# Single steps for constants, gates, head norms and turns, and VectorE for the rotation's sum

## The reference

```python
oa = diff_attention(...)      # group 0: two softmaxes per head, p0 - lam*p1; rms_norm of the output
ob = window_attention(...)    # group 1: rope, band mask, sink, 2 key heads
on = neighborhood_attention(...)  # group 2: relative bias, 4 key heads
od = qknorm_attention(...)    # group 3: rms_norm of q and k, rope, 2 key heads
y = (jnp.concatenate([oa, ob, on, od], axis=-1) * jax.nn.silu(p[12])) @ w_out[l]

def apply_rope(x, cos, sin):
    h = x.shape[-1] // 2
    x1, x2 = x[..., :h], x[..., h:]
    return jnp.concatenate([x1 * cos - x2 * sin, x2 * cos + x1 * sin], axis=-1)
```

## Time and profile before

| | us |
|---|---|
| median of 3 timed runs | 3154.34 (3153.6 to 3158.98) |
| profiled execution, its own time | 3150.2 |
| its span | 3148.0 |
| TensorE matmul busy | 2928.6 (93%) |
| VectorE busy | 1927.3 (61%) |
| ScalarE busy | 1166.4 (37%) |
| GpSimd busy | 385.0 (12%) |
| mean granted TensorE clock | 0.953 of full speed |

### The profile page before, as it was taken

How to read it: one execution, slowest core, us unless ns; L and a number is a source line. 1 busy time by engine, 2 the same in 40 slices (tenths; PEclk the granted TensorE clock), 3 DMA queues, 4 the chain that set the end, 5 groups by cost and what they waited for, 6 DMA issues and landing times. The chain is left out here.

```text
span 3148.0 us, 40440 instructions
## 1 busy us (share of the span) xinstructions
PE 2928.6 (93%) x15557; PEld 2369.7 (75%) x15557; DVE 1927.3 (61%) x3369; ACT 1166.4 (37%) x1870; POOL 385.0 (12%) x365
## 2 busy tenths in 40 slices
PE   7979899999889996999998998989999999999998
PEld 2447578777667874868776787765789999999886
DVE  3228778676776767262434557886776666666444
ACT  3233332323223334242433444233344444444443
POOL 5760000000100001000000002542410000000000
PEclk9989999999899998999999998995799999999999
DMA  9836235343344664323332353430244555555554
GB/s 339 278 138 238 84 133 197 112 163 121 110 161 148 207 224 151 114 91 112 118 106 96 119 182 126 141 112 22 79 145 151 187 182 182 183 181 188 195 188 156
DMA packets 154592, 484.79 MB, mean 154 GB/s; under 512 B 17168, under 2 KB 18192, under 8 KB 153232
## 3 DMA queue, kind: packets, MB, share of 16 engines
q1 hardware_dynamic: 139968, 439.42, 41.4%
q10 hardware_dynamic: 14432, 42.79, 3.9%
HBM read 469.03 MB, written 13.11 MB: 153 GB/s over the span
## 5 line engine op out<-in xcount | busy, mean ns | idle before, releaser
L1457 DVE TENSOR_TENSOR split_weights<-common,split_weights 128x1024 fp32r<-128x1024 f32 x644 | 798.0, 1247 | 666.3 <-ACT split_weights L2166 611.3
L2166 ACT ACTIVATE split_weights<-common 128x1024 fp32r<-128x1024 f32 x644 | 671.6, 1052 | 829.5 <-PE bank L1133 777.0
L1131 PE MATMUL bank<-split_weights,features 128*128 128x512 f32 x1920 | 806.2, 420 | 27.8 <-DVE split_weights L1457 11.3
L1133 PE MATMUL bank<-split_weights,features 128*128 128x512 f32 x1920 | 759.7, 396 | 0.0
L1132 PE MATMUL bank<-split_weights,features 128*128 128x512 f32 x1920 | 759.3, 395 | 0.0
L1131 PEld LDWEIGHTS bank<-split_weights,features 128*128 128x128 f32 x1920 | 368.4, 192 | 137.7 <-issue 44.3
L1132 PEld LDWEIGHTS bank<-split_weights,features 128*128 128x128 f32 x1920 | 368.7, 192 | 79.3 <-issue 11.3
L1133 PEld LDWEIGHTS bank<-split_weights,features 128*128 128x128 f32 x1920 | 366.6, 191 | 80.6
L1131 PE MATMUL bank<-ffn_input_split,split_weights 128*128 128x256 f32 (+1 forms) x1376 | 389.1, 283 | 0.8 <-issue 0.8
L1133 PE MATMUL bank<-ffn_input_split,split_weights 128*128 128x256 f32 (+1 forms) x1376 | 388.2, 282 | 0.0
L1132 PE MATMUL bank<-ffn_input_split,split_weights 128*128 128x256 f32 (+1 forms) x1376 | 387.7, 282 | 0.0
(11 more groups left out here) (296 smaller groups left out, 3429.5 us busy)
## 6 DMA issues: line engine op xcount, KB each, us to landing
common<-w_in SPq DMA_DIRECT2D x260, 512.0 KB, 3.3
common<-w_up SPq DMA_DIRECT2D x172, 512.0 KB, 4.3
first_block_work<-w_mod_cols SPq DMA_DIRECT2D x256, 256.0 KB, 3.7
common<-w_out SPq DMA_DIRECT2D x104, 512.0 KB, 3.3
common<-w_down SPq DMA_DIRECT2D x84, 512.0 KB, 3.3
old_stream<-w_mod SPq DMA_DIRECT2D x64, 512.0 KB, 5.1
trig<-common ACTq DMA_DIRECT2D x32, 272.0 KB, 5.0
second_block_work<-trig ACTq DMA_DIRECT2D x32, 272.0 KB, 2.7
```

The source lines that it names most:

```text
L1131: e.matmul(out_ap, xs[0], ws[0], start=first, stop=False)
L1133: return e.matmul(out_ap, xs[0], ws[1], start=False, stop=last)
L1457: e.tensor_tensor(lo, raw, hi.bitcast(F32), ALU.subtract).then_inc(*low_done.tick(("lo", m)))
L2166: e.activation(split_slots[:, 0, i, 0:words], raw_slots[:, m % RAW, 0:words], ACT.Copy).then_inc(*high_done.tick(("high", m)))
```

## The change

Four composite steps are taken apart. `layer_consts` becomes `lambda_sums`, `lambda_exp`, `lambda_made` and four `bias_mask` steps, put 20 to 48 sides after the constants' load; the lambda products are written over their own input rather than into a turn buffer. `gate` becomes `gate_tanh` (ScalarE, at the finish) and `gate` (VectorE, two sides later). `norm_heads` becomes `square_heads` (squares, mean, power) at the finish and `norm_heads` with `rotate_heads` two sides later, with two buffers for the means. `heads_out` of group 0 keeps the mean and the power; `heads_scaled`, issued after the next scores, does the scalings and frees bank 7.

The end of q no longer forces the pending turns: it issues the attention that is left and nothing else. Head tiles of group 0's first q and k in layer 0 are turned 20 sides after their finish in place of 3 or 8. Squares and rotations have each their own turn buffer.

In `rotate_heads` the first sine product is multiplied by -1 in the same instruction (a scalar_tensor_tensor), and VectorE adds the whole product tile to the cosine tile in one instruction; GpSimd's two instructions are gone.

```diff
@@ -218,8 +218,8 @@
 
 PACE, LAST_PACE = (0.36, 0.45), (0.65, 0.8)
 SCAN_PACE = 0.5
-CONTEXT_AFTER = 4
-TURN_AFTER = dict(copy=3, turn=8, norm=14)
+CONTEXT_AFTER, GATE_AFTER, NORM_AFTER = 4, 2, 2
+TURN_AFTER = dict(first=20, copy=3, turn=8, norm=14)
 
 
...
@@ -282,11 +283,22 @@
 
     def later(self, sides, *step):
         self.delayed.append((self.clock + sides, step))
+        self.delayed.sort(key=lambda d: d[0])
+
+    def late(self):
+        step = self.delayed.pop(0)[1]
+        if step[0] == "gate":
+            self.scale_heads()
+        self.do(*step)
+
+    def flush(self):
+        while self.delayed:
+            self.late()
 
     def side(self, work=1.0):
         self.clock += 1
         while self.delayed and self.delayed[0][0] <= self.clock:
-            self.do(*self.delayed.pop(0)[1])
+            self.late()
         if self.turned:
             if self.turned[0][0] < self.clock:
                 self.do(*self.turned.pop(0)[1])
...
@@ -493,16 +505,17 @@
             self.staged += 1
             self.stage_before[r], self.stage_now[t] = self.stage_now[t], ("staged", r)
             self.stage_last[(l, t)] = ("staged", r)
-            after = "copy"
+            after = "first" if l == 0 and g == 0 else "copy"
             if kind == "qk":
                 self.scratch += 1
-                self.do("norm_heads", l, g, part, nh, p, t, bank, r, self.turns(), self.scratch)
+                self.do("square_heads", l, nh, p, t, bank, r, self.turns(0))
+                self.later(NORM_AFTER, "norm_heads", l, part, nh, t, r, self.scratch)
                 if t < LT:
-                    self.do("rotate_heads", l, nh, "head", p, t, bank, r, self.turns(), self.scratch)
+                    self.later(NORM_AFTER, "rotate_heads", l, nh, "head", p, t, bank, r, self.turns(1), self.scratch)
                 after = "norm"
             elif t < LT and ROPE[kind]:
-                self.do("rotate_heads", l, nh, ROPE[kind], p, t, bank, r, self.turns(), None)
-                after = "turn"
+                self.do("rotate_heads", l, nh, ROPE[kind], p, t, bank, r, self.turns(t % 2), None)
+                after = "first" if l == 0 and g == 0 else "turn"
             else:
                 self.do("copy_heads", l, g, part, nh, p, t, bank, r)
             self.turned.append((self.clock + TURN_AFTER[after], ("turn_heads", l, g, part, nh, t, r)))
...
@@ -545,13 +559,21 @@
                 t, h = units[i - 2]
                 self.do("values", first + i - 2, l, g, kvh, t, h)
                 if h == HEADS - 1:
+                    self.flush()
                     r = None
                     if ("gate", l, g, t) in self.reached:
                         r = self.rows()
                     else:
                         self.reached.add(("output", l, g, t))
                     self.do("heads_out", first + i - 2, l, g, kind, t, r)
+                    if kind == "diff":
+                        self.unscaled.append(("heads_scaled", first + i - 2, l, g, t, r))
             yield
+        self.scale_heads()
+
+    def scale_heads(self):
+        while self.unscaled:
+            self.do(*self.unscaled.pop())
 
     def gate(self, l, g):
         def finish(p, t, bank):
...
@@ -560,7 +582,8 @@
                 r = self.rows()
             else:
                 self.reached.add(("gate", l, g, t))
-            self.do("gate", l, g, p, t, bank, r)
+            self.do("gate_tanh", l, g, p, t, bank, r)
+            self.later(GATE_AFTER, "gate", l, g, p, t, bank, r)
         return finish
 
     def y_rows(self, l, c, at):
...
@@ -581,7 +604,8 @@
                         self.project(tiles[LT:], self.heads(l, g, kind, "k", HEADS))
                 elif part == "q":
                     self.project(qtiles, self.heads(l, g, kind, "q", HEADS))
-                    self.side_all()
+                    while self.side_work:
+                        self.advance(self.side_work)
                 elif part == "k":
                     self.project(tiles, self.heads(l, g, kind, "k", HEADS))
                 elif part == "v":
...
@@ -591,9 +615,11 @@
                 if g == 0 and part == "q":
                     self.scratch += 1
                     self.do("load_layer_consts", l, self.scratch)
-                    mask_at = self.scratch
-            if g == 0:
-                self.do("layer_consts", l, mask_at, self.turns())
+                    self.later(20, "lambda_sums", l)
+                    self.later(26, "lambda_exp", l)
+                    self.later(32, "lambda_made", l)
+                    for h in range(HEADS):
+                        self.later(36 + 4 * h, "bias_mask", l, h, self.scratch)
             self.side_work.append(self.attention(l, g, kind, kvh, qtiles))
             self.pace = PACE[l] if place < 3 else LAST_PACE[l]
             self.project(qtiles, self.gate(l, g))
...
@@ -1630,36 +1657,40 @@
             e.tensor_tensor(feat[:, 1, f, 0:nt * P], tb[:, 0:nt * P], feat[:, 0, f, 0:nt * P].bitcast(F32), ALU.subtract).then_inc(
                 *features_made.tick(("feature", "mixed", l, f, 0), ("feature", "mixed", l, f, 1), ("free", "mixed", l, f)))
 
-        def layer_consts(l, z, x):
-            m = scratch.rearrange("p (t k) -> p t k", k=LAT)
+        def bias_mask(l, h, z):
             for s, n in seen.new(at("bias", l), at("mask", l)):
                 e.wait_ge(s, n)
-            for h in range(HEADS):
-                b = na_bias[:, h * LT:(h + 1) * LT, :]
-                names = [("na_ready", l), ("scratch", z)] * (h == HEADS - 1)
-                e.tensor_tensor(b, b, m, ALU.add).then_inc(*constants_made.tick(*names))
+            b = na_bias[:, h * LT:(h + 1) * LT, :]
+            names = [("na_ready", l), ("scratch", z)] * (h == HEADS - 1)
+            e.tensor_tensor(b, b, scratch.rearrange("p (t k) -> p t k", k=LAT), ALU.add).then_inc(*constants_made.tick(*names))
+
+        def lambda_sums(l):
             lv = lam_words.rearrange("p (v d) -> p v d", d=SUB)
-            prod = (turn_a, turn_b)[x % 2][:, 0:2 * SUB].rearrange("p (v d) -> p v d", d=SUB)
-            for s, n in seen.new(at("lambdas", l), at("turn", x - 2)):
-                e.wait_ge(s, n)
-            e.tensor_tensor(prod, lv[:, 0:3:2, :], lv[:, 1:4:2, :], ALU.mult).then_inc(*constants_made.tick())
+            for s, n in seen.new(at("lambdas", l)):
+                e.wait_ge(s, n)
+            e.tensor_tensor(lv[:, 0:3:2, :], lv[:, 0:3:2, :], lv[:, 1:4:2, :], ALU.mult).then_inc(*constants_made.tick())
             e.wait_ge(*constants_made.last())
-            e.tensor_reduce(lam_t[:, 0:2], prod, AX.X, ALU.add).then_inc(*constants_made.tick(("lambda_sums", l)))
+            e.tensor_reduce(lam_t[:, 0:2], lv[:, 0:3:2, :], AX.X, ALU.add).then_inc(*constants_made.tick(("lambda_sums", l)))
+
+        def lambda_made(l):
             for s, n in seen.new(at("lambda_exp", l)):
                 e.wait_ge(s, n)
             e.tensor_tensor(lam_col, lam_t[:, 2:3], lam_t[:, 3:4], ALU.subtract).then_inc(*constants_made.tick())
             e.wait_ge(*constants_made.last())
             e.tensor_scalar(lam_col, lam_col, 0.8 - 0.6 * math.exp(-0.3 * l), None, ALU.add).then_inc(
-                *constants_made.tick(("lambda", l), ("turn", x)))
-
-        def norm_heads(l, g, part, nh, p, t, bank, r, x, z):
-            w = nh * HD
-            src, hs, gain = stage[t][:, 0:w], hss[:, 0:nh], 0 if part == "q" else 1
+                *constants_made.tick(("lambda", l)))
+
+        def square_heads(l, nh, p, t, bank, r, x):
+            w, hs = nh * HD, head_sums[r % 2][:, 0:nh]
             for s, n in seen.new(at("head_squares", r)):
                 e.wait_ge(s, n)
             e.tensor_reduce(hs, h3((turn_a, turn_b)[x % 2][:, 0:w]), AX.X, ALU.add).then_inc(*heads_made.tick(("turn", x)))
             e.wait_ge(*heads_made.last())
             e.tensor_scalar(hs, hs, 1.0 / HD, EPS, ALU.mult, ALU.add).then_inc(*heads_made.tick(("head_means", r)))
+
+        def norm_heads(l, part, nh, t, r, z):
+            w = nh * HD
+            src, hs, gain = stage[t][:, 0:w], head_sums[r % 2][:, 0:nh], 0 if part == "q" else 1
             for s, n in seen.new(at("head_power", r), at("scratch", z - 1)):
                 e.wait_ge(s, n)
             e.tensor_tensor(h3(scratch[:, 0:w]), h3(src), bc(hs, 2, (P, nh, HD)), ALU.mult).then_inc(*heads_made.tick())
...
@@ -1686,9 +1717,13 @@
             e.tensor_tensor(a, v, cos, ALU.mult).then_inc(*heads_made.tick())
             for s, n in seen.new(at("turn", x - 2)):
                 e.wait_ge(s, n)
-            e.tensor_tensor(b[:, :, 0, :], v[:, :, 1, :], sin, ALU.mult).then_inc(*heads_made.tick())
+            e.scalar_tensor_tensor(out=b[:, :, 0, :], in0=v[:, :, 1, :], scalar=-1.0, in1=sin, op0=ALU.mult, op1=ALU.mult).then_inc(
+                *heads_made.tick())
             names = [("free", "acc", p, t)] if z is None else [("scratch", z)]
```

(47 more changed lines are left out.)

51 lines of the change are left out of this document (27 added, 24 removed).

## The result

The changed kernel takes 3111.6 us (median of 4, 3109.5 to 3112.07), the kernel before on the same chip 3153.97 (4 runs, 3150.27 to 3158.98): ratio 0.9863, interval 0.9846 to 0.988, 42.4 us faster. Forecast were 3097, 57 us faster. The profiled execution of the changed kernel spans 3110.3 us, 37.7 less than before's.

What follows compares the result with a forecast made beforehand. TensorE, busy 93% of the span, was taken as the bound (at most some 220 us to be had). Seven terms summed to 57.1 us, span 3148.0 to 3090.9; with 2.2 and 4.1 added, 3097 us, range 3060 to 3125.

Steps and rivals of the forecast that it cites:

- 1 first turns: Layer 0's first head turns: later turns let TensorE restart sooner after its 14.1 us wait; 6.7 us gained, bounds 4 to 8.
- 2 constants: First attention, layer 0: masks and lambda in single steps shorten VectorE's lateness; 2.5 us gained, bounds 0 to 8.
- 3 difference heads: Difference attention's tile ends: later scaling brings the combination sooner, 0.4 us at each of six; 2.5 us, bounds -3 to 9.
- 4 window group, layer 0: Layer 0's window group: key products fill the gap after q as far as VectorE follows; 5.4 us, bounds 2 to 10.6.
- 5 norm group, layer 0: Layer 0's norm group: the gap after q fills as far as VectorE's queue shortens; 11 us, bounds 5 to 22.7.
- moved pieces: Seven modulation pieces moved to later stages shift one load of c rows into the stream's end; ±2 us, taken as 0.
- 6 layer 1: Layer 1's three ends of q: VectorE has room, so the gaps really fill; 28 us gained, bounds 20 to 31.
- step 7: Turns of copied heads after q, now spread; 1 us gained.
- the stalls move: Rival, 3118 us, chance 0.24: in layer 0 TensorE waits the same later, at the end of kv or a weight split.
- all gaps fill: Rival, 3068 us, chance 0.14: VectorE catches up while TensorE works; layer 0's window and norm groups give 33.3 us, not 16.4.
- The sums: All 24 rotations, with sums moved from GpSimd, were charged as 15.1 us more work for VectorE.
- The slower rival: Rival, 3188 us, chance 0.07: the gate frees its accumulator two steps later, delaying projections at 24 gate tiles, 91 us.

Runs made afterwards that it cites:

- Experiments 2: The kernel before with one part alone: the end of q no longer forces the turns, sums stay on GpSimd; 3132.57 us, ratio 0.9927.
- experiment 4: The changed kernel with `side_all` back at the end of q, forcing the turns again; 3136.38 us, ratio 0.9939 to the kernel before.
- experiment 3: The changed kernel with the sums of the rotated heads back on GpSimd; 3115.89 us, ratio 0.9875 to the kernel before.
- experiment 12: The kernel before with 64 modulation pieces held back to layer 1 and one piece in 4 sides in layer 0; 3120.88 us, ratio 0.9892.
- Experiment 7: The changed kernel with 1, 3 and 5 modulation pieces put in at layer 0's three ends of q; 3117.19 us, ratio 0.9881.
- Experiment 8: The changed kernel with the last 64 modulation pieces (layer 1's gates) held back until layer 1's attention; 3092.84 us, ratio 0.9808.
- experiment 11: The changed kernel with the last 64 modulation pieces held back and one piece in 4 sides instead of 3 without attention work; 3059.44 us, ratio 0.9694.
- experiment 9: The changed kernel with the difference heads scaled at once, in the step of the heads' output; 3117.38 us, ratio 0.9874.
- experiment 10: The changed kernel with the gate's second half and the norm due at the next side, not two later; 3115.99 us, ratio 0.9872.

## Why the prediction was right, and where it was off

By its own steps, in us of the two profiled spans (37.7 in all; the medians differ by 42.4). Each is the rise in the changed kernel's column between two products.

| step | forecast | measured | between products |
|---|---|---|---|
| 1 first turns | 6.7 | 4.9 | start to 129 |
| 2 constants | 2.5 | 1.7 | 183 to 202 |
| 3 difference heads | 2.5 | 1.6 | 202 to 276 |
| 4 window group, layer 0 | 5.4 | 4.7 | 520 to 697 |
| 5 norm group, layer 0 | 11 | 6.5 to the end of kv, 11.1 to the attention's | 697 to 837, to 896 |
| moved pieces | 0 (±2) | -11.9 | 896 to 1183 |
| 6 layer 1 | 28 | 24.9 | 1183 to 1796 |

What is left: -0.4 from 129 to 183, 2.6 from 276 to 520 (the copied heads' turns of step 7, forecast 1, and further difference heads), and -1.5 after the attention.

The measured 3111.6 lies inside the stated range of 3060 to 3125, but 1.6 above the forecast's own 3085 to 3110, and nearer to the rival "the stalls move" (3118) than to 3097. That is chance: this rival gives terms 2 to 5 nothing, and they gave 19.1 us (forecast 21.4). A loss that no term of the sum held brought the total down to it.

**The mechanism held.** Experiments 2 and 4 show it from both sides: letting q end without its forced turns is worth 20 to 25 us, the rest of the change 17 to 19 (experiment 4 against its before). The size that steps 4 and 5 set, what TensorE keeps if VectorE must follow, came out too: 15.8 us by the attention's end for 16.4 forecast, with 12.4 of 34.0 us given back in the norm group's kv. The rival "all gaps fill" wanted 33.3 us from them. It was wrong for this kernel, and no less for the paced one, where the change gives these two groups 15.3 us. So 16 pieces fewer (150 for 166 at product 896) did not make the change worth more there, nor did the sums taken off VectorE in experiment 3 (16.2 us). VectorE's work is on TensorE's path in these groups in both kernels: the pacing alone gives 18.3 us from product 520 to 896 (experiment 12). That it is also what stops the gaps from filling rests on the waits shown, for VectorE or for ScalarE behind VectorE, and not on an experiment.

**The step that failed is "The seven pieces moved to later ... ±2, taken as 0".** They came to 9 by product 896 (175 against 166), not seven, each of two passes, and the term cost 11.9 us. I had credited steps 4 and 5 with the pieces that leave, and not debited the stage that they go to. The code's order told where: the output projection, in which VectorE is busy 147.07 of 204.12 us before and waits 33.4 us for the next pieces' loads from 985 to 1215. Experiment 4 removes the loss by bringing back the whole old order. Experiment 7, which brings back the number of pieces and not their places, shows two parts: about 6.9 us with the moved pieces, and 4.2 with the one that stands ahead of the features. Experiment 8 shows that the stage is better off still without the last 64. Of the 6.2 us c-row load only its new place and the longer wait (10.52 for 7.24) are shown; I did not try the load alone.

**Step 6 was too high in its first group:** 5.9 (14.3 to 20.2) where 9.9 were forecast. The column reaches 24.9 at product 1186 and loses 4.7 at once. VectorE, still at the features, rotates late, and TensorE stops 2.03 us and runs slow:

```profile
1237.79 0.41 DVE L1720 SCALAR_TENSOR_TENSOR common<-bank,first_block_work 128x256 f32<-128x256 f32 x1
1238.12 0.41 DVE L1723 TENSOR_TENSOR common<-bank,first_block_work 128x256 f32<-128x256 f32 x1
...
1238.59 0.50 PE L1158 MATMUL bank<-split_weights,features 128*128 128x512 f32 x1 [2.03 <-DVE common L1723]
```

In experiment 11, with no pieces there, the same group rises from 65.6 to 75.2, 9.6 us. The window group's 5.4 (forecast 4.0) and the norm group's 12.8 (14.4) are right.

**Small terms.** Step 1 was 1.8 high, of which 1.4 is that later stage: taken from there, the restart comes 4.8 us sooner, as forecast, and the slow stretch remained. The sums cost about what I charged: 14.5 us for all 24 against 15.1, a wide one taking 0.69 us, while VectorE's busy time as a whole rose by 10.5. The sine product with the turned sign took as long as the plain one behind it (0.415 us both, 128x256). Step 3's price was shown by experiment 9, by place and not in the total (2.7 us, mine 2.5), with the wait for the scaling at the values that I named. The slower rival, the gate's late accumulator, did not appear: the products wait 0.4 us once behind its line 1850, and experiment 10 without the delay is not faster.

**A rule that spoke against the change.** The Trainium skill, Perfetto Trace Analysis, section Optimizing Scalar/DVE Operations, says that giving work of a saturated VectorE to another engine, even GpSimd, may make sense, with the caution that the two share a read port, so that moving work between them might not help. Here the sums on GpSimd (experiment 3) came out 4 us slower if anything. Between products 520 and 896, where VectorE is fullest, its profile gained 16.2 us and the changed kernel's 15.8, so there it made no difference, and the caution is what this case bears out. GpSimd's 128x256 sums took 1.12 and 1.04 us on the mean, the shortest 0.74 and the longest 1.74. That a port is the reason no run here shows.

## What to carry to other kernels

When an order of work is paced by a counter, taking empty steps out of it moves all that the counter pays out. Price it at the stage that it lands in, not only at the one that it leaves, look at which item now stands ahead of which reader (one piece ahead of two features: 4 to 5 us), and check whether the work was due there at all: 64 pieces that were first needed a layer later cost 17 us by being early, more than most edits of the change gave. Two changes need not add up (42 and 34 us apart, 96 together); where the surplus lies is read from the places, not from the totals. And compare two traces by when the same work is reached, since waits change their names without changing their cost (42.9 us on GpSimd became 36.1 on VectorE, for 1 to 4 us).

## What I had not expected of the hardware

Where VectorE is behind, TensorE can pay for its work in full. In experiment 11 ten pieces fewer by product 697 (118 for the changed kernel's 128) went with 16.5 us gained there (31.6 for 15.1), 1.6 us a piece. That is just what such a piece costs VectorE: two passes of 0.75 us and two reads of 0.08. VectorE was busy only 73% of layer 0's attention before the change, and still none of this work was hidden. The same ten pieces fewer in the kernel before (120 for 130, experiment 12) gained 14.6. What a piece costs is no constant, though: experiment 7 has two more than the changed kernel by product 697 and stands 6.5 us lower there (8.6 for 15.1).

TensorE's clock follows the stops. From product 896 to 1152 the granted clock averages 0.97 in the changed kernel and 1.00 in experiments 11 and 12, where TensorE's longest wait in the stage is 1.9 and 1.4 us (10.5 in the changed kernel).
